# Two gate tiles of a decoder trunk as seven block products of half width

## What is computed

```python
proj = rmsnorm(x, norm_g) @ w_in
(a_val, a_gate, a_z, q, k, v, b_z, c_b, c_c, c_x, c_z, gates) = jnp.split(proj, SPLIT_IDX, axis=-1)
...
g = sigmoid(gates + gate_b).reshape(b, s, 3, D_MODEL)
merged = g[:, :, 0] * y_a + g[:, :, 1] * y_b + g[:, :, 2] * y_c
out = rmsnorm(x + merged @ w_o, final_g)
```

## Time and profile before

| | |
|---|---|
| Median of 3 runs | 2284.22 us (2283.36 to 2284.63) |
| Profiled execution | 2282.93 us |
| its span, first to last instruction | 2281.1 us |
| TensorE busy | 99% |
| VectorE, ScalarE, GpSimd busy | 63%, 33%, 10% |
| DMA, mean over the span | 216 GB/s, 493.53 MB |
| Granted TensorE clock | 0.999 |

### The profile page before, as it was taken

The page is one execution under the profiler, slowest core; times in us unless marked ns, Lnnn a source line. Parts: engine busy times, 40 slices in busy tenths (PEclk is TensorE's granted clock), DMA queues, the critical chain, the costliest instruction groups (busy, mean ns, idle before and its releaser), DMA issues.

```text
span 2281.1 us, 29046 instructions
## 1 busy us (share of the span) xinstructions
PE 2257.2 (99%) x10822; PEld 1832.9 (80%) x10822; DVE 1426.0 (63%) x2706; ACT 756.0 (33%) x1610; POOL 232.8 (10%) x186
## 2 busy tenths in 40 slices
PE   7999999999999999999999999999999999999998
PEld 6888888878888888888788788888877787788886
DVE  4767667764666665564557667665556657677752
ACT  4333332342333331032344344102135455441121
POOL 3544400100000000010000000001000000000010
PEclk9999999999999999999999999999999999999999
DMA  8877788798566665566755565556765555545555
GB/s 315 288 265 265 270 289 290 273 342 321 166 203 183 181 175 183 190 254 238 263 185 170 166 199 156 169 196 239 257 258 144 179 161 168 156 136 183 187 193 201
DMA packets 99339, 493.53 MB, mean 216 GB/s; under 512 B 15360, under 2 KB 18304, under 8 KB 54144
## 3 DMA queue, kind: packets, MB, share of 16 engines
q1 hardware_dynamic: 90464, 488.90, 63.8%
q10 hardware_dynamic: 8736, 2.78, 0.6%
HBM read 378.37 MB, written 113.27 MB: 216 GB/s over the span
## 4 chain that ended last, share of the span: by engine, by line
PE 96%; DVE 2%; DMA 1%; issue 1%; ACT 0%; SPq 0%; DVEq 0%; ACTq 0%
PE PJ L769 75%; PE SC L828 6%; PE SC L860 5%; PE TB L869 3%; PE OB L893 1%; PE OB L894 1%; PE OB L828 1%; PE PJ L828 1%; PE OB L896 1%; PE OB L895 1%; PE TB L904 0%; DMA Wraw<-w_stream 0%; DMA PX<-x_t 0%; PE TB L920 0%; PE SC L769 0%
## 5 line engine op out<-in xcount | busy, mean ns | idle before, releaser
L769 PE MATMUL PJ<-hT,Wp 128*128 128x512 f32 x6480 | 1571.4, 394 | 0.5 <-DVE PX L1632 0.5
L769 PEld LDWEIGHTS PJ<-hT,Wp 128*128 128x128 f32 x6480 | 1189.5, 188 | 254.0 <-issue 17.7
L1552 DVE SCALAR_TENSOR_TENSOR ACCS<-UA,col,ACCS 128x512 f32<-128x512 f32 x464 | 350.7, 798 | 0.4
L1066 ACT ACTIVATE PX<-SC,negm 128x512 f32<-128x512 f32 (+3 forms) x320 | 196.2, 623 | 145.5 <-DVE negm L1381 143.6
L1426 DVE TENSOR_TENSOR ZA<-TB,ZA 128x512 fp32r<-128x512 f32 (+1 forms) x144 | 95.1, 660 | 177.0 <-ACT ZA L1086 176.0
L1381 DVE TENSOR_REDUCE negm<-SC 128x2 f32<-128x1024 f32 (+3 forms) x160 | 169.0, 1061 | 40.3 <-PE SC L860 37.6
L1086 ACT ACTIVATE ZA<-TB 128x512 fp32r<-128x512 f32 (+1 forms) x144 | 82.6, 574 | 321.8 <-PE TB L869 321.8
L1137 ACT ACTIVATE TG<-PJ,col 128x512 f32<-128x512 f32 x64 | 44.1, 690 | 351.2 <-PE PJ L769 351.2
L1419 DVE SCALAR_TENSOR_TENSOR PX<-PX,sc 128x512 f32<-128x512 f32 (+3 forms) x160 | 108.0, 695 | 51.0 <-ACT PX L1077 50.8
L828 PE MATMUL SC<-Wp,KM 128*128 128x512 f32 x384 | 121.5, 389 | 0.0
L1077 ACT ACTIVATE PX<-PX,sc 128x512 f32<-128x512 f32 (+3 forms) x160 | 98.9, 655 | 64.9 <-DVE sc L1408 44.6
(11 more groups left out here) (192 smaller groups left out, 2037.4 us busy)
## 6 DMA issues: line engine op xcount, KB each, us to landing
Wp<-split_weights SPq DMA_DIRECT2D x264, 1024.0 KB, 4.8
split_weights<-Wp SPq DMA_DIRECT2D x88, 1024.0 KB, 4.9
Wraw<-w_stream SPq DMA_DIRECT2D x88, 512.0 KB, 5.9
KM<-keys SPq DMA_DIRECT2D x24, 512.0 KB, 5.9
VM<-values SPq DMA_DIRECT2D x24, 512.0 KB, 6.5
PX<-x SPq DMA_DIRECT2D x16, 512.0 KB, 7.6
out<-PX SPq DMA_DIRECT2D x16, 512.0 KB, 10.6
keys<-KM SPq DMA_DIRECT2D x12, 512.0 KB, 9.5
```

The costliest lines, as they stand in the source:

```text
L769: mm = pe.matmul(pj(c, r)[:, :], wt, rhs[:, 1 if q == 1 else 0, k, :], start=(n == 0), stop=(n == 3 * ktiles - 1))
L1066: a = act.activation(probs(c, h, t, j, m)[:, 0:w], SC[k][:, m, 0:w], ACT.Exp, bias=negm[:, t % 2, j, m:m + 1], accum_out=lsum[:, t % 2, j, ...
L1552: a = dve.scalar_tensor_tensor(out=acc, in0=src, scalar=col[:, n:n + 1], in1=acc, op0=ALU.mult, op1=ALU.add)
```

## The change

In chunks 1 to 3 the two gate tiles of one `m` are computed together. The channels of `hT` are cut in two halves of 512, its rows in two halves of 256, and the 1024x256 weights of both tiles are a 2x2 matrix of blocks A11 (gate b, first channels), A12 (gate b, last), A21, A22 (gate c). The 2x2 product is formed from seven block products in place of eight (Strassen-Winograd form), each 4 channel blocks x 3 passes = 12 matmuls of 256 columns, 7 of them to a step: weights A11, A12, A22 and four sums S1 to S4, against blocks of `hT` and four sums of them. What is new for it:

- *Quarters.* Each product goes to half a bank of `SC`. ScalarE copies the first one (`copy_first`); VectorE adds the seven into quarters of `TG` (`add_quarter`, 128x256); tanh then works in place in `TG`. Products wait for `quarter_done` where a bank is used again.
- *Weight blocks.* `Wp` has six slots of half a tile. A11, A12, A22 come raw (256 KB) and are split each time (`block_hi`, `block_lo`). S1 to S4 are made once, in the heads of chunk 1 (VectorE `weight_sum`, ScalarE, GpSimd, one every 7 steps), stored, and loaded split (512 KB). They pass through two rooms (`SS`). The gate tiles are not stored in chunk 0 any more.
- *Sums of the activations.* At steps 510 to 521 of a chunk VectorE makes four sums out of the next chunk's rows (`turned_sums`), they are split and stored (2 x 2 MB), and loaded into `KM` and `VM` when these are free: behind the last scores (step 272) and behind the last `times_v` (step 304 to 306).
- *Steps moved.* More taps in the heads, the layernorm and the next rows' loads and work some steps over; other rooms for attention's pairs.

```diff
-HEAD_TAPS = (58, 46, 24, 0)
+HEAD_TAPS = (58, 72, 78, 50)
-AFTER_FROM = 268
+AFTER_FROM = 272
-LN_AT = (408, 408, 408, 414)
+LN_AT = (400, 408, 408, 408)
-LN_SPREAD_AT = 13
+LN_SPREAD_AT = 15
-X_LOAD_AT = (436, 440)
-XN_AT = (452, 444, 444, 0)
-XT_AT = (469, 461, 461, 0)
+XN_AT = (456, 454, 454, 0)
+XT_AT = (471, 467, 467, 0)
+RAW_AT = ((0, 0, -14), (0, 1, -13), (1, 1, -9))
+SPLIT_AT = ((A11, -6), (A12, -5), (A22, 0))
+QUARTER_AT = (6, 7, 7, 10, 10, 12, 12)
+BLOCK_AT = ((S1, -9), (S2, -7), (S3, -3), (S4, 0), (YB, 4), (YC, 6))
+SUM_AT = 24
+SUM_STEP = 7
+SUMS_AT = 510
+SUMS_STORE_AT = (20, 40)
+X_LOAD_AT = ((442, 444), (446, 448), (446, 448))
+SUMS_BACK_AT = 272
...
+        P_BANKS = {A11: SC[0][:, 0, 0:HALF], S1: SC[0][:, 1, 0:HALF], S2: SC[1][:, 0, 0:HALF], A12: SC[1][:, 1, 0:HALF],
+                   S3: SC[0][:, 0, 0:HALF], S4: SC[1][:, 0, 0:HALF], A22: SC[1][:, 1, 0:HALF]}
...
+            def gates_part(c, m, part):
+                n0 = merge_at(c, m)
+                for n in range(PRODUCTS * part, PRODUCTS * (part + 1)):
+                    b, i = divmod(n, 3 * KB)
+                    k, q = divmod(i, 3)
+                    if i == 0:
+                        weight_ready(c, mid_block(m, b))
+                        if b == A11:
+                            wait(pe, quarter_done, PRODUCTS * (n0 - 1) + 4)
...
+                        elif b == S3:
+                            pe.wait_ge(p1_copied, n0 + 1)
+                            if m == 0:
+                                pe.wait_ge(t_back[1], 64 * c)
+                        elif b == S4:
+                            pe.wait_ge(quarter_done, PRODUCTS * n0 + 1)
+                        elif b == A22:
+                            pe.wait_ge(quarter_done, PRODUCTS * n0 + 3)
+                    l = 1 if q == 1 else 0
+                    rows = {A11: hT[:, l, k, 0:HALF], S1: TS[:, l, k, 0:HALF], S2: TS[:, l, k, HALF:],
+                            A12: hT[:, l, KB + k, 0:HALF], S3: TU[:, l, k, HALF:], S4: hT[:, l, KB + k, HALF:],
+                            A22: TU[:, l, k, 0:HALF]}[b]
+                    mm = pe.matmul(P_BANKS[b], Wp[:, block_slot(c, mid_block(m, b)), 1 if q == 2 else 0, k * P:(k + 1) * P], rows,
+                                   start=(i == 0), stop=(i == 3 * KB - 1))
...
+            def add_quarter(c, m, k):
+                n = merge_at(c, m)
+                b, src, dst, after = ((S2, P1[:, :], C22, 0), (S1, C22, C12, 1), (A12, P1[:, :], C11, 0), (S3, C22, C21, 1),
+                                      (S1, C21, C22, 4), (S4, C12, C12, 2), (A22, C21, C21, 4))[k]
+                dve.wait_ge(prod_done, PRODUCTS * n + b + 1)
...
+                dve.tensor_tensor(dst, P_BANKS[b], src, ALU.add).then_inc(quarter_done, 1)
```

More of the change, by code:

```diff
@@ L67 @@
 G_CHUNK = G_YA + M_OUT
-BANK_CHUNK = G_CHUNK // 2
+BANK_CHUNK = (G_CHUNK - 2 * M_OUT) // 2
+GROUPS = G_CHUNK - 2 * M_OUT
+PRODUCTS = 7
+A11, S1, S2, A12, S3, S4, A22, YB, YC = range(9)
+MID_BLOCKS = 9
+B_MID = 2 * W_MID
+B_YA = B_MID + MID_BLOCKS * M_OUT
+B_FIN = B_YA + M_OUT
+B_CHUNK = B_FIN + 2 * WO_T
+B_FIRST = 2 * W_CHUNK
 def bank(r):
@@ new lines, in merge_tile, with gate_tile, block_before, count_tables @@
+def merge_tile(i):
+    return W_MID <= i < W_YA
+def gate_tile(i):
+    return merge_tile(i) and (i - W_MID) % 3 < 2
+def block_before(c, q):
+    n = block_at(c, q) - SLOTS
+    if n < B_FIRST:
+        return 0, n
+    c, q = divmod(n - B_FIRST, B_CHUNK)
+    return c + 1, q
+def count_tables():
+    low, stored, back = {}, {}, {}
+    stores, backs, n = [0] * SLOTS, [0] * SLOTS, 0
+    for i in range(W_CHUNK):
+        n += 1
+        low[0, 2 * i] = low[0, 2 * i + 1] = n
+        if not gate_tile(i):
+            s = block_slot(0, 2 * i)
+            stores[s] += 1
+            stored[i] = (s, stores[s])
+    for c in range(1, NCHUNK):
+        units = [(2 * i, 2) for i in range(W_MID)]
+        units += [(mid_block(m, k), 1) for m in range(M_OUT) for k in range(MID_BLOCKS)]
+        units += [(tile_block(c, i), 2) for i in range(W_YA, W_CHUNK)]
+        for q, size in units:
+            if B_MID <= q < B_YA and (q - B_MID) % MID_BLOCKS in (A11, A12, A22):
+                n += 1
+                low[c, q] = n
+            else:
+                s = block_slot(c, q)
+                backs[s] += 1
+                for k in range(size):
+                    back[c, q + k] = (s, backs[s])
+    return low, stored, back
@@ new lines, with raw_table @@
+LOW, STORED, BACK = count_tables()
+RAW_HALVES = 4
+def raw_table():
+    order = [(0, i, a) for i in range(W_CHUNK) for a in range(2)]
+    for m in range(M_OUT):
+        g = W_MID + 3 * m
+        order += [("sum", g + 1, 0), ("sum", g + 1, 1), ("sum", g, 0), ("sum", g, 1)]
+    for c in range(1, NCHUNK):
+        for m in range(M_OUT):
+            g = W_MID + 3 * m
+            if c == 1 or m > 0:
+                order += [(c, g, 0), (c, g, 1), (c, g + 1, 1)]
+    table, loads = {}, [0] * RAW_HALVES
+    for n, half in enumerate(order):
+        room = n % RAW_HALVES
+        if half[0] != 0 or half[2] == 0:
+            loads[room] += 1
+        table[half] = room, loads[room]
+    for c in range(2, NCHUNK):
+        for n, (i, a) in enumerate(((0, 0), (0, 1), (1, 1))):
+            table[c, W_MID + i, a] = RAW_HALVES + n, c - 1
+    return table, order
@@ L339, in room_table @@
 def room_table(c):
-    free = [(r, None) for r in range(SPARE if c == 0 else 4 * KB)]
+    free = [(r, None) for r in range(SPARE[c] if c < 2 else 4 * KB)]
     room, last = {}, {}
@@ L604, in build @@
+        C11, C12, C21, C22 = [TG[:, i, j * HALF:(j + 1) * HALF] for i in range(2) for j in range(2)]
         block = ctx.enter_context(nc.Block())
@@ L692, in _ @@
                          lam_v[0:1, :].to_broadcast([P, 256])).then_inc(lam_in, 16)
-            for w in range(W_SLOTS):
+            for w in range(3):
                 store_split(w)
```

526 lines of the change are left out of this document (416 added, 110 removed).

## The result

The changed kernel takes **2290.9 us** (median of 5 runs, 2283.62 to 2293.64) against 2283.8 (5 runs, 2283.22 to 2284.63) before: ratio 1.0024, 95% interval 1.0014 to 1.0035: a quarter of a percent slower, small but clear of no change. The kernel before ran beside every set and took 2283.5 to 2284.2; all ratios are to it. The times spread by 10 us where those of before spread by 1.4; that is itself a finding. The profiled execution took 2283.62 (span 2281.7) and is the fastest of its five, so it shows only part of the loss. The rest is read from a second profile of the same kernel, that of experiment 2 (2295.68). They are called the first and the second execution here.

A forecast was written before the change was run, and what follows sets the result against it. TensorE, busy in 99% of the span, was taken as the bound. Terms -23.2 + 1.7 + 3 + 3 + 3 = -12.5 us from 2282.93 gave 2270.4, plus 1.3 for the median 2271.7, stated as 2271; 8-in-10 range 2252 to 2291.

The forecast's parts named there:

- the third rival: VectorE in the heads: a fifth of 126 us moved in delays attention's transposes, +25 in place of +3, 2294; chance 0.13.
- (1): Gate matmuls: 84 narrow at 0.118 us replace 48 wide at 0.2267 per pair, gaining 23.2 us over 24 pairs.
- The lower bound: Gate matmuls: a narrow one at 0.1133 us, half a wide one, which would gain 32.7 us.
- The upper bound's "debt": Gate matmuls: some 0.02 us that two narrow ones may pass to wide ones behind, making 0.125 us each.
- (2): Each product's two waits, for block and bank: 0.01 us at 168 starts, 1.7 us; bounds 0 to 8.4.
- (3): Products waiting for VectorE's adds: covered, except in the layernorm stretch; 1 us a chunk, 3 us in all.
- (4): Heads: moved taps and chunk 1's 32 weight sums bring VectorE to 73 to 77%; 3 us, bounds 0 and 25.
- the 1550 predicted: VectorE's total busy time in the changed kernel: about 1550 us, as 1426 + 72 + 22 + 30.
- (5): Loading activation sums: values' part may delay S3, 1 us a chunk, 3 us; keys' part has 36 us.
- (6): Weight-block loads, 255 GB/s per pair and 292 in chunk 1's heads: nothing taken, bounds 0 and 5 us.
- "7 us or more in hand": Loads queued on SyncE behind sum blocks waiting for room: each was said to have 7 us or more.
- (7): Chunk 0: 16 stores fewer, layernorm 8 steps earlier, x row loads later: covered by the output stage, nothing.

The follow-up runs named there:

- experiment 2: The changed kernel again, without an edit, for a second profile and its spread: 2295.07 us, ratio 1.0042 to the kernel before.
- run 9: Changed kernel, complete, with VectorE turning the scales in 32x32 blocks and two DMAs storing 4 x 128 bytes each: 2276.70 us, ratio 0.9972.
- run 1: Separate kernel, nothing of the reference: six streams of 96 matmuls, each with its own weight load, 512 to 128 columns; 0.120 us each at 256.
- run 6: Changed kernel with the first weight tile behind the merge stage asked for after the last YC block: 2291.23 us, ratio 1.0031.
- run 3: Changed kernel with the taps back in the merge stage, the weight sums kept: 2311.22 us, ratio 1.0121.
- run 5: Changed kernel with a quiet store: the 21 scale stores write one 1 KB row of zeros instead of 256 x 4 bytes; 2277.09 us, ratio 0.997.
- run 4: Changed kernel without chunk 1's weight sums (none made or stored; sum blocks loaded from other stored weights): 2282.91 us, ratio 0.9995.
- Run 11: run 9 plus run 6's edit, second-pair raw halves (chunks 2, 3) and x rows (chunks 1, 2) later, chunk 0's steps mostly restored: 2271.36 us, ratio 0.9947.
- run 12: Changed kernel with the scales stored as 128 packets of 8 bytes in place of 256 of 4: 2276.62 us, ratio 0.9972.

## Why the prediction was wrong

I said 2271, faster. It is 2290.9, slower, at the very end of the range, and near the third rival (2294), though not by its mechanism. The miss of 19.9 us is 3.8 from the spacing of narrow matmuls (1) and some 14 from loads held up behind the stores (6, seen through 4 and 5). The other losses come to some 12.3 us (2276.7 of run 9, less 2283.8, plus 19.4) where the prediction had 10.7; that these are close is luck, since they stand at other places than the ones that were costed. By the steps:

**(1) Matmuls: the direction was right, the term mis-sized.** I took 0.118 between 0.1133 and 0.120, though the two nearest rows both said 0.12. A row that is there beats a proportion that no row shows: -19.4, not -23.2. The lower bound, half of a wide one, wasn't possible, since 13 ns per matmul don't shrink (run 1). The upper bound's "debt" didn't exist either. This is 3.8 us of the miss.

The Trainium skill (TensorE: Matmul & The Clock Gate, section Back-to-back issue gap) has a sustained spacing of 131 ns for 512 columns with a load each, and columns / 2.4 + 2.5 ns for one alone. No stream of fp32r here goes by the first; the second has the right slope and 11 ns too little (0.2267, 0.120).

**(2) Waits at products:** predicted +1.7, measured 0 (even distances of 1.44 us).

**(3) Banks and quarters:** predicted +3, measured some 0.3 per chunk (run 6 has 127.5 in chunk 1's merge stage, and 133.7 - 8 x 0.81 is 127.2). TensorE's list has no wait for a quarter in the changed kernel. In run 3, with VectorE busy for 56.91 of 59 us, the waits that I feared appear, at the places named.

**(4) Taps and weight sums in the heads:** predicted +3; the heads cost +9.3 in the first execution, and those of chunk 1 alone +22.2 in the second. The step asked how full VectorE would be, and 77% is indeed harmless (run 5: +1.3 in chunk 1, with all taps and sums in place). What it didn't ask is **what the new instructions wait for**. A tap waits for nothing; a sum of weights waits for a raw half that DMA brings, and stands in a fixed order in front of attention. Moving taps was right (run 3), and putting an instruction with a DMA in front of it there is what cost. VectorE's total came out 27 us above the 1550 predicted; 20 of these are slower taps (last section).

**(5) Sums of the activations:** I looked for the cost at S3, and it is next to nothing: TensorE's list of waits has no entry there in the merge stages of chunks 1 and 2, and 0.3 us are lost in chunk 3. The keys' part, that "has 36 us", I costed at nothing: it had enough for itself, but the weight tiles queued behind 2 MB of it on SyncE hadn't once a hold-up came on top. In run 4 that is the whole loss in the heads (7.8 us); in run 5, with the same 2 MB and the quiet store, TensorE has no wait there.

**(6) Weight blocks: the step that failed most.** I took nothing, with bounds of 0 and 5 us, for raw halves, sum blocks and weight tiles that come late, from mean rates: 292 GB/s wanted, 281 seen. The runs showed some 14 us in its place (run 9 against the changed kernel). The mean is the wrong view. The trace of before had stretches of 8 us at 47 GB/s, which averages of 71 and 302 us don't show. Anything that DMA brings there has to have those 8 us in hand. The order within SyncE's queue cost another 1.1 to 1.6 us in each chunk's last pair (YC), and with the first pair of chunk 3 some 1.7, where I had "7 us or more in hand" and hadn't counted L879's wait for a slot ahead of the block.

**(7) The rest:** predicted 0. Chunk 0 costs +3.2: the normalising of the next rows now falls between the products of branch a's outputs, and TensorE waits for VectorE's CT at four places (2.7 us against 1.1). Run 11 puts the steps back: the outputs of chunk 0 lose 0.6 in place of 2.1, the merge stage 0 in place of 0.5. Its heads there are 1.5 over before, where nothing was changed back, and they vary from -0.1 to +1.7 among the executions of the changed kernel and its variants; why is open.

The rival that came nearest, VectorE in the heads, had the right stage and the wrong reason. That the engine was too full is refuted by runs 5 and 9, which keep all its work; its waits are real but end at a DMA. The loss was split in run 4 only in one execution: what of the 22 us goes to raw halves and what to weight tiles isn't known for a median run. That the times scatter fits a loss that hangs on whether a hold-up meets a load with little in hand, but which runs meet how many wasn't counted.

## What to carry to other kernels

Before costing a new load by mean bandwidth, go through the trace of before in stretches of a few microseconds and look for those in which the DMA share is high and GB/s low: their length is what each load has to have in hand. Here a store of many tiny packets stood ahead of each one that was looked at. Judge a remedy by the same short stretches and not by the time alone: run 12's time says that the hold-up is gone, and its trace that it is half as long. When work is moved to an engine with room, ask of each instruction what it waits for; one that waits for DMA makes everything behind it wait as well, however idle the engine is. A hidden defect of a kernel can be free until a change takes the slack away, so the same remedy may be worth nothing before and 14 us after.

## What the runs showed of the hardware

- **A store of 256 packets of 4 bytes (1 KB) holds up the loads behind it for some 8 us.** 37 to 80 GB/s with the DMA engines recorded as busy, against 150 to 295 in the same stretches with another form of the store. With 128 packets of 8 bytes it is some 4 us (74 GB/s against 219 with the quiet store), with 8 of 128 bytes none is seen. The store's own packets are recorded with 9 ns each; it is 8 KB packets of loads behind them that are recorded with up to 7 us in place of 0.31. What these wait for stays open. The Trainium skill (DMA: Bandwidth & Descriptors, section Why small descriptors are slow (HBM only)) tells of a fixed overhead of about 3 cycles per packet, 27% at 256 bytes. A cost that goes with the number of packets fits run 12, but one of that size, within the small packets themselves, is not where this trace shows the time.
- **A wait of TensorE can cost twice.** Behind a wait of 5.6 us twelve wide matmuls took 4.95 us in place of 2.72, granted clock 0.50 at first; the same behind four waits of 1.8 to 3.3 us in the second execution, 1.7 us each. Waits of 1.79 and 1.90 us in the first execution and of 1.92 in the second left the clock at 1.00, so the length of the wait alone doesn't tell.
- **A matmul with its own weight load is spaced columns / 2.4 GHz + 13 ns** from 512 to 256 columns (within 3 ns, fp32r, clock 1.00), and 0.111 us at 128, though the load is recorded with 188 ns.
- **Taps became slower where GpSimd works beside them:** 841 ns at the mean in place of 798 for the same 464 instructions, 464 x 0.043 = 20 us more of VectorE. Sorted by whether a GpSimd instruction overlaps them, the taps without one take 745 ns in both kernels, and those with one 1.10 us before and 1.08 after. Of the latter there are 70 before and 132 after, which makes 20 us: the whole difference. GpSimd is busy for 385 us in place of 233. The changed kernel's line:

```profile
L2044 DVE SCALAR_TENSOR_TENSOR ACCS<-UA,col,ACCS 128x512 f32<-128x512 f32 x464 | 382.7, 841 | 0.8
```
